# The projection phase of a hybrid encoder layer: new orders around the projections, and squares averaged per head by two single-pass products

## The chip, the core and the metric

The kernel runs on one core of a Trainium2 chip. Five engines work side by side, each through its own queue in order, and wait for one another by semaphores: TensorE (PE) for matrix products, VectorE (DVE), ScalarE (ACT), GpSimd (POOL), and SyncE (SP), which here issues every DMA. The metric is the time of the whole program on the device in microseconds (us).

## The reference, cut to what matters

One encoder layer is applied to a prompt of 1024 tokens and to a sample of 512 tokens, each with 16 learned meta tokens ahead. All in float32, to float32 accuracy.

```python
h = _rmsnorm(x, norm1_g)
proj = h @ w_in                                   # 1024 -> 2304 columns
qa, ka, va, qb, kb, vb = jnp.split(proj, SPLITS, axis=-1)
qa = _rmsnorm(qa.reshape(B, L, NA_HEADS, HEAD_DIM), qn_a_g)   # per head of 64; ka, qb, kb alike
...
mix = jnp.concatenate([_rmsnorm(oa, outn_a_g), _rmsnorm(ob, outn_b_g)], axis=-1)
x = x + mix @ w_out
h = _rmsnorm(x, norm2_g)
x = x + (jax.nn.silu(h @ w_gate) * (h @ w_up)) @ w_down
```

The change is in the projection and in the per-head normalization of queries and keys, which needs the mean of the squares over each head's 64 numbers.

## The kernel before

**Products in three passes.** A float32 number is split into a high part (rounded to the type `fp32r`, in which TensorE makes a product in one pass) and the low rest. `product` (lines 396 to 398) adds high x high, low x high and high x low in a PSUM bank.

**The stages.** A norm phase normalizes and transposes the first 512 tokens and the meta tokens. Then come `project(0)` (these tokens), `project(1)` (prompt tokens 512 to 1023), the prompt's attention, `project(2)` (the sample), the sample's attention, the output projection and the feed-forward network. g is the group of tokens, 0 to 2.

**One group.** `project(g)` has 18 half-steps H. Each takes 128 columns of `w_in` over 512 tokens: 8 x 3 products of 512 columns on PE (in group 0 from H=8 on, 48 smaller ones, since the meta tokens go along). H=0 to 7 are queries; then K and V alternate, H=8 K, H=9 V, and so on to H=16 K, H=17 V. A query or K half-step is "normed":

- ACT `take_out(H)`: waits for PE's half-step H (`mm_done`), makes the high part `wh` of the weights of H+2 (line 1235), waits that DVE has finished H-2 (`normed`), and copies the bank to `raw` and its square to `sq` (lines 1266, 1267).
- POOL `weight_lo`: the low part `wl` of the same weights (line 1044).
- PE `after(g, H)`, after half-step H+1: the head average of the squares, a plain float32 product of `sq` with the 128x128 matrix `head_mean` (line 2203).
- ACT `root(H)`, in half-step H+1 behind that half-step's `take_out`: square root (line 1300).
- DVE `divide(H)`: reciprocal (line 1706), then times `raw` and gain (line 1715).

V half-steps are copied, transposed on PE (lines 2213, 2217) and split; a K is split by `key_high` and `key_low` (lines 1317, 1734) a step later.

**The tokens of the next groups** are prepared inside groups 0 and 1, four tiles x0 to x3 and x4 to x7. In half-steps 0, 2, 4, 6 ACT takes the norm (`x_root`) and DVE scales the tile (`norm_scale`, line 1667), behind that half-step's `divide`. In half-steps 1, 3, 5, 7 PE transposes it (`x_turn`, line 2159), behind `after`, and ACT copies it out. At H=16 of group 0 ACT and DVE split the next group's tokens into `hth` and `htl` (lines 1247, 1740), behind `key_high` and `key_low`.

**Weights** are loaded into two buffers, by SP, when POOL has done the weights before them. The load for H=2 of group 0 stands behind the norm phase's end and the position tables' DMAs.

The order on PE is this loop:

```python
            def project(g):
                for H in range(18):
                    products(g, H)
                    if H:
                        after(g, H - 1)
                    elif g == 1:
                        after(0, 17)
                    n = prepared(g, H)
                    if n is not None and H % 2:
                        x_turn(n)
```

## Time and profile before

| what | value |
|---|---|
| median of 3 runs | 1973.41 us (1971.73 to 1975.48) |
| the profiled execution's own time | 1974.77 us |
| its span, first to last instruction | 1973.0 us |
| mean granted TensorE clock | 0.979 of full |
| PE busy | 1862.0 us, 94% of the span |
| DVE / ACT / POOL busy | 66% / 51% / 48% |
| products of the tokens with the input weights, first to last on PE | 34.0 to 623.7 us, the prompt's attention among it |

The profiled execution is one run and is read instruction by instruction; its span and the 1.8 us around it make its time, which stands 1.4 us above the median. A busy share is an average. What a stage is bound by is seen from its waits: which instruction came last, and whom it held up.

### The profile page before, as it was taken

What the parts mean: (1) busy time and instruction counts of PE and PEld (TensorE: products, weight loads), DVE (VectorE), ACT (ScalarE), POOL (GpSimd) and SP (SyncE); (2) the same over time, 40 slices, a digit from 0 to 9 for tenths busy, and PEclk for the clock granted to TensorE, in tenths of its full rate; (3) what the DMA queues carried; (4) which work ended last, traced back from release to release, by engine and by line L of the source; (5) the groups of instructions that cost most, each with busy time, mean ns of one, the idle gap of its engine ahead of it and who ended that gap; (6) DMA issues with size and microseconds to landing.
All of it is one profiled execution on the core that took longest, in us unless ns stands there. A gap on an engine that the chain in (4) does not pass through costs nothing.

```text
span 1973.0 us, 35334 instructions
## 1 busy us (share of the span) xinstructions
PE 1862.0 (94%) x12047; PEld 1673.4 (85%) x12047; DVE 1298.4 (66%) x2349; ACT 1003.6 (51%) x2085; POOL 953.7 (48%) x807
## 2 busy tenths in 40 slices
PE   5897998999898988997999999999999999999998
PEld 3696777999777876886899999899999989999997
DVE  2556657888666876548666666776666676666664
ACT  3546446888545883345444344544435353444432
POOL 1332335766435652113656464645546464655643
PEclk9999998999998998998999999999999999999999
DMA  4444622444423445011332332343233234323221
GB/s 139 138 134 126 166 85 78 128 126 133 123 77 93 140 119 205 32 54 64 122 114 87 104 106 85 107 172 123 90 106 106 86 107 171 107 92 121 85 85 64
DMA packets 184323, 217.10 MB, mean 110 GB/s; under 512 B 13124, under 2 KB 162100, under 8 KB 183964
## 3 DMA queue, kind: packets, MB, share of 16 engines
q1 hardware_dynamic: 184220, 215.77, 34.9%
q8 instruction: 60, 0.98, 0.2%
q14 instruction: 43, 0.35, 0.1%
HBM read 197.34 MB, written 27.27 MB: 114 GB/s over the span
## 4 chain that ended last, share of the span: by engine, by line
PE 56%; DVE 4%; ACT 2%; issue 2%; POOL 1%; DMA 0%; ACTq 0%; POOLq 0%; DVEq 0%; SPq 0%
PE bank L396 19%; PE bank L397 18%; PE bank L398 18%; DVE mvl L1991 1%; POOL msl L1107 1%; ACT msh L1477 0%; DVE tsum L1987 0%; ACT logit L1383 0%; DVE qm L1888 0%; ACT qm L1407 0%; DVE logit L1813 0%; DMA draw<-in_w_down 0%; DVE pmeta L1828 0%; ACT pth L1392 0%; DVE ptl L1820 0%
## 5 line engine op out<-in xcount | busy, mean ns | idle before, releaser
L396 PE MATMUL bank<-mvh,sth 128*128 128x256 f32 x1848 | 526.2, 285 | 16.3 <-DVE mvl L1991 6.0
L398 PE MATMUL bank<-mvh,stl 128*128 128x256 f32 x1848 | 525.2, 284 | 0.0
L397 PE MATMUL bank<-mvl,sth 128*128 128x256 f32 x1848 | 525.2, 284 | 0.0
L396 PEld LDWEIGHTS bank<-mvh,sth 128*128 128x128 f32 x1848 | 356.6, 193 | 19.6 <-issue 15.0
L397 PEld LDWEIGHTS bank<-mvl,sth 128*128 128x128 f32 x1848 | 357.0, 193 | 1.2
L398 PEld LDWEIGHTS bank<-mvh,stl 128*128 128x128 f32 x1848 | 356.9, 193 | 0.0
L1184 POOL TENSOR_TENSOR dl<-draw,dh 128x1024 fp32r<-128x1024 f32 x66 | 158.2, 2422 | 366.0 <-ACT dh L1570 366.0
L2029 DVE TENSOR_TENSOR y<-bank,y 128x512 f32<-128x512 f32 x264 | 182.4, 692 | 165.4 <-PE bank L398 164.5
L1044 POOL TENSOR_TENSOR wl<-wraw,wh 128x1024 fp32r<-128x1024 f32 x54 | 134.3, 2488 | 269.1 <-ACT wh L1235 269.1
L1178 POOL TENSOR_TENSOR stl<-graw,sth 128x512 fp32r<-128x512 f32 x132 | 177.1, 1343 | 101.8 <-ACT sth L1552 97.5
L396 PE MATMUL bank<-dh,acth 128*128 128x512 f32 x528 | 210.1, 398 | 7.7 <-DVE y L2029 5.3
L397 PE MATMUL bank<-dl,acth 128*128 128x512 f32 x528 | 209.1, 396 | 0.0
L398 PE MATMUL bank<-dh,actl 128*128 128x512 f32 x528 | 208.4, 395 | 0.0
L396 PE MATMUL bank<-hth,wh 128*128 128x512 f32 (+2 forms) x512 | 199.9, 390 | 6.5 <-DVE htl L1740 5.5
L1586 ACT ACTIVATE acth<-act_f 128x512 fp32r<-128x512 f32 x66 | 38.2, 624 | 322.3 <-PE bank L398 314.3
L398 PE MATMUL bank<-hth,wl 128*128 128x512 f32 (+2 forms) x512 | 187.4, 366 | 0.0
L397 PE MATMUL bank<-htl,wh 128*128 128x512 f32 (+2 forms) x512 | 186.4, 364 | 0.0
L1178 POOL TENSOR_TENSOR stl<-uraw,sth 128x512 fp32r<-128x512 f32 x132 | 169.9, 1315 | 5.7 <-ACT sth L1552 5.7
L1235 ACT ACTIVATE wh<-wraw 128x1024 fp32r<-128x1024 f32 x54 | 57.0, 1057 | 188.1 <-PE bank L398 163.6
L1383 ACT ACTIVATE logit<-logit,negm 128x274 f32<-128x274 f32 (+1 forms) x192 | 113.8, 593 | 38.0 <-DVE negm L1813 36.8
L1706 DVE RECIPROCAL rt_p<-rt_p 128x512 f32<-128x512 f32 (+2 forms) x30 | 84.4, 2826 | 67.6 <-ACT rt_p L1300 67.6
L396 PEld LDWEIGHTS bank<-dh,acth 128*128 128x128 f32 x528 | 99.9, 189 | 31.1 <-DVE y L2029 6.5
(247 smaller groups left out, 4293.5 us busy)
## 6 DMA issues: line engine op xcount, KB each, us to landing
graw<-in_w_gate SPq DMA_DIRECT2D x33, 1024.0 KB, 5.4
uraw<-in_w_up SPq DMA_DIRECT2D x33, 1024.0 KB, 5.3
draw<-in_w_down SPq DMA_DIRECT2D x66, 512.0 KB, 4.1
wraw<-in_w_in SPq DMA_DIRECT2D x54, 512.0 KB, 4.0
bias_rows<-table_a SPq DMA_DIRECT2D x36, 192.0 KB, 3.2
out<-y SPq DMA_DIRECT2D x12, 512.0 KB, 3.1
bias<-table_b SPq DMA_DIRECT2D x28, 201.0 KB, 2.6
table_a<-line_a_dram SPq DMA_DIRECT2D x8, 576.0 KB
```

Of the source, the lines that this page charges most:

```text
L396: pe.matmul(out, lhs[0], rhs[0], start=start, stop=False, skip_group_check=True)
L397: pe.matmul(out, lhs[0], rhs[1], start=False, stop=False, skip_group_check=True)
L398: return pe.matmul(out, lhs[1], rhs[0], start=False, stop=stop, skip_group_check=True)
L1044: pool.tensor_tensor(wl[G % 2][:, :, :], wraw[G % 2][:, :, :], f32(wh[G % 2][:, :, :]), ALU.subtract).then_inc(w_lo, 1)
L1107: pool.tensor_tensor(msl[slot][:, :, :], mix_tile(i, slot), f32(msh[slot][:, :, :]), ALU.subtract).then_inc(ms_lo, 1)
L1178: pool.tensor_tensor(stl[:, i, :, :], standing(raw, i), f32(sth[:, i, :, :]), ALU.subtract).then_inc(st_lo_pool, 1)
L1184: pool.tensor_tensor(dl[j][:, :], draw[j][:, :], f32(dh[j][:, :]), ALU.subtract).then_inc(down_lo, 1)
L1235: act.activation(wh[G % 2][:, :, :], wraw[G % 2][:, :, :], ACT.Copy).then_inc(w_hi, 1)
L1383: act.activation(x, x, ACT.Exp, bias=negm[:, h % 2, t:t + 1], scale=-1.0, accum_out=lsum[:, h % 2, t:t + 1]).then_inc(expd, 1)
L1586: act.activation(acth[:, j, :], act_f[:, j, :], ACT.Copy).then_inc(act_hi, 1)
L1706: op = dve.reciprocal(rt[:, u0:u0 + w], rt[:, u0:u0 + w])
L2029: dve.tensor_tensor(yt, DOWN_BANK[half][:, :], yt, ALU.add).then_inc(y_add, 1)
```

## The change

Four things are done.

1. **Squares.** Behind `sq`, ACT copies it to `sqh` in `fp32r`, waiting for its own square first. POOL makes `sql = sq - sqh`, behind its `weight_lo` of the same half-step. PE's head average becomes two `fp32r` products, `sqh` and `sql` with `head_mean_r` (the matrix in `fp32r`; its entries are 0 and 1/64), and waits for `squared_lo`, POOL's result.
2. **Next tokens.** `norm_scale` moves to half-steps 1, 3, 5, 7 in group 0 and 3, 5, 7, 9 in group 1; `x_turn` to the half-step after each, 2 to 8 and 4 to 10. Their loads and the write-back of the turned tiles move along.
3. **Weights.** The loads for half-steps 2 and 3 of group 0 are issued before the norm phase ends, and the first load of each group waits for one buffer only.
4. **The seam between groups 0 and 1.** Of the eight slices of the next tokens' low part DVE makes the even ones and POOL the odd ones, POOL's ahead of its `sql`. `key_high(0, 14)` and `key_low(0, 14)` move between slices 3 and 4.

```diff
@@ -96,6 +96,7 @@
...
     head_mean = r("head_mean", [P, P])
+    head_mean_r = at("head_mean_r", [P, P], F32R, r.offset - P * 4)
     eps = r("eps", [P, 1])
@@ -152,11 +153,13 @@
...
     assert BASE + s.offset <= END
-    sq_of, rt_of = [], []
+    sq_of, sqh_of, sql_of, rt_of = [], [], [], []
     for n, where in (("p", qm_at[2]), ("s", v_at + 4 * 1280 * 4)):
...
         rt_of.append([s(f"rt_{n}{i}", [P, SEG + META]) for i in range(2)])
+        sqh_of.append([s(f"sqh_{n}{i}", [P, SEG + META], F32R) for i in range(2)])
+        sql_of.append([at(f"sql_{n}{i}", [P, SEG + META], F32R, where + i * 4 * (SEG + META)) for i in range(2)])
@@ -431,9 +438,15 @@
...
-        def prepared(g, H):
-
-            return 4 * g + H // 2 if g < 2 and H < 8 else None
+        def squared_x(g, H):
+
+            j = (H - (1, 3)[g]) // 2 if g < 2 and H % 2 else -1
+            return 4 * g + j if 0 <= j < 4 else None
+
+        def turned_in(g, H):
+
+            j = (H - (2, 4)[g]) // 2 if g < 2 and H % 2 == 0 else -1
+            return 4 * g + j if 0 <= j < 4 else None
@@ -450,6 +463,12 @@
...
             return sq_of[g // 2], rt_of[g // 2]
+
+        def squares_split(g, kind):
+            return ([sqh_kv], [sql_kv]) if g and kind == "kvb" else (sqh_of[g // 2], sql_of[g // 2])
+
+        def square_columns(g, kind):
+            return SEG + META if g == 0 and kind != "q" else SEG
@@ -794,23 +813,25 @@
...
             def weight_loads(g):
-                if g == 0:
-                    sp.wait_ge(line_out, 16 * 7)
                 for it in range(1, 9):
+                    if g == 0 and it == 2:
+                        sp.wait_ge(line_out, 16 * 7)
+                        lay_out_a0(0)
                     kind, i = ("q", it) if it < 4 else ("kv", it - 4) if it < 8 else ("kvb", 0)
                     for slot in range(2):
-                        sp.wait_ge(w_lo, 18 * g + it * 2 + slot - 1)
-                        weight_load(kind, slot, i)
-                        if g == 0 and slot == 1:
+                        if g or it > 1:
+                            sp.wait_ge(w_lo, 18 * g + it * 2 + slot - 1)
+                            weight_load(kind, slot, i)
+                        if g == 0 and slot == 1 and it > 1:
                             lay_out_a0(it - 1)
...
                             lay_out_b(2 * it + slot - 2)
-                    if g < 2 and it in (2, 3):
-                        later_x(4 * g + it)
-                    if g == 0 and it in (6, 7):
-                        later_x(it - 2)
-                    if g == 1 and 2 <= it < 6:
-                        keep_turned(it - 2)
+                    if g == 0 and it in (3, 4, 6, 7):
+                        later_x(it - 1 if it < 5 else it - 2)
+                    if g == 1 and it in (4, 5):
+                        later_x(it + 2)
+                    if g == 1 and 4 <= it < 8:
+                        keep_turned(it - 4)
@@ -830,6 +851,9 @@
...
                 norm_rest()
+                for slot in range(2):
+                    sp.wait_ge(w_lo, slot + 1)
+                    weight_load("q", slot, 1)
                 later_x(0)
@@ -955,8 +979,9 @@
...
-            sp.wait_ge(w_lo, 18)
-            first_weights(1)
+            for slot in range(2):
+                sp.wait_ge(w_lo, 17 + slot)
+                weight_load("q", slot, 0)
             weight_loads(1)
@@ -1048,6 +1073,18 @@
...
                         weight_lo(18 * g + H + 2)
+                    if g == 0 and H == 16:
+                        for k in range(1, KT, 2):
+                            pool.wait_ge(h_hi, k + 1)
+                            pool.tensor_tensor(htl[:, k, 0:SEG], qm[:, 1, k, :], f32(hth[:, k, 0:SEG]),
+                                               ALU.subtract).then_inc(h_lo_pool, 1)
+                    if is_normed(H):
+                        kind, i, slot = half_step(H)
+                        w = square_columns(g, kind)
+                        sqh, sql = squares_split(g, kind)
+                        pool.wait_ge(squared_hi, normed_of(g, H))
+                        pool.tensor_tensor(sql[slot][:, 0:w], squares(g, kind)[0][slot][:, 0:w],
+                                           f32(sqh[slot][:, 0:w]), ALU.subtract).then_inc(squared_lo, 1)
@@ -1266,6 +1303,10 @@
...
                     op.then_inc(squared, 1)
+                    act.wait_ge(squared, normed_of(g, H))
+                    w = square_columns(g, kind)
+                    act.activation(squares_split(g, kind)[0][slot][:, 0:w], sq[slot][:, 0:w], ACT.Copy
+                                   ).then_inc(squared_hi, 1)
                     return
@@ -1354,27 +1395,30 @@
...
                         value_high(0, 17)
-                    if H >= 2 and half_step(H - 2)[0] != "q" and slot == 0:
-                        key_high(g, H - 2)
-                    elif g == 1 and H == 0:
-                        key_high(0, 16)
                     if g == 0 and H == 16:
...
                         for k in range(KT):
+                            if k == 4:
+                                key_high(0, 14)
                             if k < KT - 1:
...
                             split_high(1, k)
+                    elif H >= 2 and half_step(H - 2)[0] != "q" and slot == 0:
+                        key_high(g, H - 2)
+                    elif g == 1 and H == 0:
+                        key_high(0, 16)
                     if g and H == 16:
...
                             stage_q(h, False)
-                    n = prepared(g, H)
-                    if n is not None:
-                        x_out(n) if H % 2 else x_root(n)
+                    if squared_x(g, H) is not None:
+                        x_root(squared_x(g, H))
+                    if turned_in(g, H) is not None:
+                        x_out(turned_in(g, H))
@@ -1654,6 +1698,7 @@
...
                     dve.tensor_scalar(gains[:, j:j + 1], gains[:, j:j + 1], SCALE, None, ALU.mult)
+                dve.tensor_copy(head_mean_r[:, :], head_mean[:, :])
                 for k, c0 in enumerate(range(0, LEN_T5, 512)):
@@ -1756,15 +1801,17 @@
...
                         value_low(0, 17)
-                    if H >= 2 and half_step(H - 2)[0] != "q" and H % 2 == 0:
+                    if g == 0 and H == 16:
+                        for k in range(0, KT, 2):
+                            if k == 4:
+                                key_low(0, 14)
+                            split_low(1, k)
+                    elif H >= 2 and half_step(H - 2)[0] != "q" and H % 2 == 0:
                         key_low(g, H - 2)
...
                         key_low(0, 16)
-                    if g == 0 and H == 16:
-                        for k in range(KT):
-                            split_low(1, k)
-                    n = prepared(g, H)
-                    if n is not None and H % 2 == 0:
+                    n = squared_x(g, H)
+                    if n is not None:
                         if n == 0:
@@ -2180,7 +2227,10 @@
...
                             if g and H == 0:
-                                pe.wait_ge(h_lo, 8 * (g - 1) + k + 1)
+                                if g == 1 and k % 2:
+                                    pe.wait_ge(h_lo_pool, k // 2 + 1)
+                                else:
+                                    pe.wait_ge(h_lo, k // 2 + 1 if g == 1 else 4 + k + 1)
                             op = part(k, u0, w, b)
@@ -2189,7 +2239,7 @@
...
                     j = normed_number(g, kind, slot, i)
-                    pe.wait_ge(squared, j + 1)
+                    pe.wait_ge(squared_lo, j + 1)
                     if g == 2 and H == 0:
@@ -2224,9 +2276,8 @@
...
                         after(0, 17)
-                    n = prepared(g, H)
-                    if n is not None and H % 2:
-                        x_turn(n)
+                    if turned_in(g, H) is not None:
+                        x_turn(turned_in(g, H))
                 if g:
```

How that stands on the engines. First ACT, group 0, half-step 3 and the start of the next. `raw`, `sq` are bank and square, `rt` the root, `xs_turned` PE's transposes. Before:

```order
30 L1235 ACTIVATE wh1_79<-wraw1_81 128x1024 [waits w_in1,mm_done]
31 L1266 ACTIVATE raw1_85<-bank1 128x512
32 L1267 ACTIVATE sq_p1_90<-bank1 128x512
33 L1300 ACTIVATE rt_p0_91<-bank4,eps_51 128x512 [waits mean_done]
34 L1341 ACTIVATE qm_62<-bank6 128x4x128 [waits xs_turned]
35 L1341 ACTIVATE qm_62<-bank7 128x4x128 [waits xs_turned]
36 L1235 ACTIVATE wh0_78<-wraw0_80 128x1024 [waits w_in0,mm_done]
```

And now, half-step 2 and the start of the next:

```order
37 L1303 ACTIVATE raw0_85<-bank0 128x512 [waits normed]
38 L1304 ACTIVATE sq_p0_90<-bank0 128x512
39 L1308 ACTIVATE sqh_p0_94<-sq_p0_90 128x512 [waits squared]
40 L1341 ACTIVATE rt_p1_93<-bank5,eps_52 128x512 [waits mean_done]
41 L1382 ACTIVATE qm_63<-bank6 128x4x128 [waits xs_turned]
42 L1382 ACTIVATE qm_63<-bank7 128x4x128 [waits xs_turned]
43 L1272 ACTIVATE wh1_80<-wraw1_82 128x1024 [waits w_in1,mm_done]
```

A copy `sqh` stands between the square and the root of the half-step before; the copy-out of the turned tile has moved by one half-step.

DVE at the start of group 0, before (`line_b` ends the norm phase; L1665 and L1667 are `norm_scale`):

```order
22 L1660 TENSOR_TENSOR line_b<-bank,band 8x14 [waits line_mm]
23 L1665 RECIPROCAL rms<-rms 128x1 [waits rms_done,gs_in,phase_done]
24 L1667 SCALAR_TENSOR_TENSOR spare<-spare,rms 128x2x512 [waits rinv_done]
25 L1706 RECIPROCAL rt_p_91<-rt_p_91 128x512 [waits root_done]
26 L1715 SCALAR_TENSOR_TENSOR qm<-raw_84,gains,rt_p_91 128x512 [waits recip_done]
27 L1706 RECIPROCAL rt_p_92<-rt_p_92 128x512 [waits root_done]
```

And now:

```order
23 L1705 TENSOR_TENSOR line_b<-bank,band 8x14 [waits line_mm]
24 L1751 RECIPROCAL rt_p_92<-rt_p_92 128x512 [waits root_done,phase_done]
25 L1760 SCALAR_TENSOR_TENSOR qm<-raw_85,gains,rt_p_92 128x512 [waits recip_done]
26 L1710 RECIPROCAL rms<-rms 128x1 [waits rms_done,gs_in]
27 L1712 SCALAR_TENSOR_TENSOR spare<-spare,rms 128x2x512 [waits rinv_done]
28 L1751 RECIPROCAL rt_p_93<-rt_p_93 128x512 [waits root_done]
```

The first `norm_scale` now stands behind the first `divide`. From then on one `norm_scale` follows every second `divide`, before and now.

POOL at the seam of groups 0 and 1, now (before, it has only the `wl` there); rows 37 and 38 are the weights of half-step 17 of group 0 and of half-step 0 of group 1:

```order
36 L1086 TENSOR_TENSOR sql_p0_96<-sq_p0_90,sqh_p0_94 128x528 [waits squared_hi]
37 L1069 TENSOR_TENSOR wl1_84<-wraw1_82,wh1_80 128x1024 [waits w_hi]
38 L1069 TENSOR_TENSOR wl0_83<-wraw0_81,wh0_79 128x1024 [waits w_hi]
39 L1079 TENSOR_TENSOR htl_89<-qm_63,hth_88 128x512 [waits h_hi] x4
40 L1086 TENSOR_TENSOR sql_p0_96<-sq_p0_90,sqh_p0_94 128x528 [waits squared_hi]
41 L1069 TENSOR_TENSOR wl1_84<-wraw1_82,wh1_80 128x1024 [waits w_hi]
```

The last `sql` of group 0 (row 40), for which PE's head average of half-step 16 waits, stands behind the four slices of `htl`.

## Rows read from the trace of the kernel before

**Rows 1.** Waits of PE, 30 to 316 us: line, released by, us in total, times, longest.

```profile
PE bank L2159 <- DVE spare L1667: 16.2, 8, 8.3
```

**Rows 2.** Timeline, PE, query half-steps of group 1: start us, us, then [idle before].

```profile
212.18 1.09 PE L2159 MATMUL bank<-ident,spare 128*128 128x128 f32 x8 [1.00 <-DVE spare L1667]
...
218.68 1.02 PE L2203 MATMUL bank<-sq_p,head_mean 128*128 128x512 f32 x2
...
219.77 0.39 PE L397 MATMUL bank<-htl,wh 128*128 128x512 f32 x1
220.00 0.39 PE L398 MATMUL bank<-hth,wl 128*128 128x512 f32 x1
```

**Rows 3.** Timeline, all engines, group 0, from the end of half-step 4.

```profile
78.14 1.02 PE L2203 MATMUL bank<-sq_p,head_mean 128*128 128x512 f32 x2
...
80.26 0.69 ACT L1300 ACTIVATE rt_p<-bank,eps 128x512 f32<-128x512 f32 x1
...
84.37 0.75 DVE L1715 SCALAR_TENSOR_TENSOR qm<-raw,gains,rt_p 128x512 f32<-128x512 f32 x1
84.55 1.02 PE L2203 MATMUL bank<-sq_p,head_mean 128*128 128x512 f32 x2
...
85.23 1.28 DVE L1667 SCALAR_TENSOR_TENSOR spare<-spare,rms 128x1024 f32<-128x1024 f32 x1
...
85.88 2.90 POOL L1044 TENSOR_TENSOR wl<-wraw,wh 128x1024 fp32r<-128x1024 f32 x1 [3.98 <-ACT wh L1235]
...
86.57 1.09 PE L2159 MATMUL bank<-ident,spare 128*128 128x128 f32 x8 [1.00 <-DVE spare L1667]
```

**Rows 4.** A copy to fp32r on ACT (timeline), and POOL's subtraction, min/median/max ns (by tile).

```profile
168.63 4.28 ACT L1247 ACTIVATE hth<-qm 128x512 fp32r<-128x512 f32 x8
...
L1178 POOL TENSOR_TENSOR stl<-graw,sth x132: 1267/1300/2260, 900.3 to 1912.1; 128x512 fp32r<-128x512 f32 x132
```

**Rows 5.** DVE beside a running POOL: timeline of the norm phase, then durations by tile.

```profile
14.35 2.35 POOL L1044 TENSOR_TENSOR wl<-wraw,wh 128x1024 fp32r<-128x1024 f32 x1 [12.85 <-ACT wh L1235]
...
15.86 1.92 DVE L1667 SCALAR_TENSOR_TENSOR xt<-xt,rms,g 128x1024 f32<-128x1024 f32 x1
...
L1734 DVE TENSOR_TENSOR kmeta<-rt_p,kmeta x12: 167/171/2222, 128.2 to 193.4; 64x16 fp32r<-64x16 f32 x12
```

**Rows 6.** Timeline, PE after idle time, and one stretch (busy us by engine, clock, DMA).

```profile
195.17 1.12 PE L2159 MATMUL bank<-ident,spare 128*128 128x128 f32 x4 [8.31 <-DVE spare L1667]
...
203.75 0.59 PE L2203 MATMUL bank<-sq_p,head_mean 128*128 128x512 f32 x1
...
1252.26 0.50 PE L396 MATMUL bank<-dh,acth 128*128 128x512 f32 x1 [2.64 <-DVE y L2029]
...
1599.77 0.80 PE L396 MATMUL bank<-dh,acth 128*128 128x512 f32 x1 [2.65 <-DVE y L2029]
...
196.00:198.00 2.00, 2.00 (x9) 1.81 (x8) 2.00 (x1) 1.19 (x2) 0.00 (x0) 0.50 0.80 264
```

**Rows 7.** Timeline, PE: last product of half-step 1; end of half-step 9, group 0.

```profile
47.41 0.40 PE L398 MATMUL bank<-hth,wl 128*128 128x512 f32 x1
...
114.97 1.05 PE L2203 MATMUL bank<-sq_p,head_mean 128*128 128x256 f32 x4
```

**Rows 8.** Timeline, PE: ends of half-steps 16, 17 (group 0), 0 and 11 (group 1).

```profile
162.47 1.04 PE L2213 MATMUL bank<-ident,raw 128*64 128x128 f32 x8
...
169.30 1.05 PE L2203 MATMUL bank<-sq_p,head_mean 128*128 128x256 f32 x4
...
178.48 0.60 PE L2213 MATMUL bank<-ident,raw 128*128 128x128 f32 x4
...
267.79 0.59 PE L2203 MATMUL bank<-sq_p,head_mean 128*128 128x512 f32 x1
```

**Rows 9.** Timeline, ACT, group 2: `raw` of half-steps 2 and 3.

```profile
531.28 0.60 ACT L1266 ACTIVATE raw<-bank 128x512 f32<-128x512 f32 x1 [0.78 <-DVE qm L1715]
...
537.15 0.60 ACT L1266 ACTIVATE raw<-bank 128x512 f32<-128x512 f32 x1 [0.24 <-DVE qm L1715]
```

16 lines of the change are left out of this document (11 added, 5 removed).

## The prediction, made before the changed kernel ran

> **What bounds the kernel now.** I read the page's busy shares first (PE 94%, so only PE's time counts), then PE's waits, then timelines around its idle stretches. Outside the projections the change touches nothing. Inside them PE runs without a gap but for three kinds of idle time. First, the eight `x_turn` wait for DVE's `norm_scale`, 16.2 us in all, 8.3 of them at one place in group 1 and 1.0 in the steady pairs [rows 1, 2]. Second, 3.4 us and a stretch of half clock after half-step 1, where ACT waited for weights. Third, some 2 us at the seam of groups 0 and 1. The sum below runs from one PE event to another; T is always the moment at which PE ends a half-step's products.
>
> **The head average.** The float32 product starts at 218.68, and the next products keep a spacing of 0.23 us [rows 2]: 219.77 - 0.23 - 218.68 = 0.86 us. Two `fp32r` products of the same width take 2 x 0.23 = 0.46. That saves 0.40 each, 39 times (13 in each group), 15.6 us on PE if PE is what is waited for. The trace has no product of this very operand pair; those of rows 2 have the same type, width and weight load, so I take 0.23, and 0.25 at most.
>
> **What the copy `sqh` adds.** ACT makes eight such copies in 4.28 us, 0.53 apart [rows 4]. Here the copy must also wait for its own square, so it can't overlap it: 0.66, bounds 0.53 and 0.8. It stands between `sq` and `root`, so `root`, `divide` and `norm_scale` come 0.66 later after T. POOL's `sql` takes 1.30 [rows 4] and stands behind `wl`: it ends near T + 5.1, and PE wants it at T + 6.0. That is hidden by the 5.55 us of products, with 0.9 us to spare.
>
> **The turn pairs, the main term.** Before, with T = 78.14 [rows 3]: `root` at T + 2.12, `divide`'s product T + 6.23 to 6.98, `norm_scale` T + 7.09 to 8.37, `x_turn` at T + 8.43. PE ends the next half-step at T2 = 84.55 = T + 6.41 (0.86 + 5.55), and POOL's `wl` starts at T2 + 1.33. Turn and 24 products take 218.68 - 212.18 = 6.50 [rows 2]. The pair of half-steps is 8.43 + 6.50 = 14.93 us.
>
> The change moves `norm_scale` and `x_turn` together, by one half-step in group 0. The distance stays: DVE scales behind the `divide` in the half-step that begins at T, PE turns one half-step later. So the 1.0 us wait is not removed. Now T2 = T + 0.46 + 5.55 = T + 6.01, `wl` is ready at T + 7.34, `divide`'s product runs T + 6.89 to 7.64, and `norm_scale` would start at T + 7.75. The order of the last two has turned over. In rows 3 `wl` came 0.65 after `norm_scale` and took 2.90 instead of its usual 2.4, ending 2.27 after DVE did. When DVE came second, it was held: a `norm_scale` of the norm phase took 1.92 beside POOL's 14.35 + 2.35 = 16.70 and ended 1.08 after it, and a 0.17 us `kmeta` took 2.22 [rows 5]. So `wl` slips in behind `divide`, ends at T + 7.64 + 2.27 = 9.91, and `norm_scale` ends at T + 10.99: `x_turn` at T + 11.05. PE is free for it at T + 6.47 and idles 4.6 us.
>
> A rule that speaks against this change: the Trainium skill (SBUF — State Buffer, "Who interferes with whom") says that a DVE instruction with two SBUF inputs and a GpSimd instruction that reads SBUF exclude each other, and that issue order decides who blocks. Rows 5 agree by their 2.22 and 1.92. If instead the two only slowed each other over their overlap, the turn would be at about T + 10 and the pair 1 us shorter; by the rule it is as computed.
>
> After such idle time the clock is at half. Behind 8.31 us of idle the granted clock was 0.50, 1.2 GHz, and the same turn and 24 products took 203.75 - 195.17 = 8.58 instead of 6.50 [rows 6]: 2.1 more. The pair becomes 11.05 + 8.58 = 19.6 us, against 14.93.
>
> **Sum, piece by piece.**
> (a) Group 0, end of half-step 1 (47.41 + 0.23 = 47.64) to end of half-step 9 (114.97) [rows 7]: 67.3 before. The weights for half-steps 2 and 3 are now there long before, so the wait at 51 us is gone; it cost about 8.7 with its half clock. Now four turn pairs, the last with 0.3 more for the meta columns: 4 x 19.6 + 0.3 = 78.7. That is **+11.4**.
> (b) Half-steps 10 to 16 of group 0: four head averages at 0.4, nothing late: **-1.6**.
> (c) Seam, from the end of half-step 16: before 178.48 - 162.47 = 16.0 [rows 8]. Now POOL makes `wl` (to +3.75), then waits for ACT's second slice (+5.3), makes four slices of 1.3 [rows 4], the last two behind ACT's `key_high`, each blocked a little by DVE's subtractions: they end near +12.1. Only then comes `sql` of half-step 16, +13.4. PE ended half-step 17 at 169.30, +6.83 [rows 8], and its head average comes ahead of group 1. It idles 6.6 us; then 0.46 + 5.55 + 2.1 for the clock: 21.5. **+5.5**. Without any blocking `sql` ends at +11.8, still 5 us late.
> (d) Group 1, end of half-step 0 to end of 11: before 267.79 - 178.48 = 89.3 [rows 8]. DVE is held by `key_low` until +13.3, then each query half-step costs the loop of (e), 6.5: the first `norm_scale`, now behind the third `divide`, ends near +33.1 (the 8.3 us wait becomes several of 0.5 to 2.3 and one of 5.6). 33.1 + 8.58 = 41.7, two pairs 39.2, and 14.5 for the last, where the V half-step has no `sqh`: 95.4. **+6.1**.
> (e) Rest: group 1 saves 3 x 0.4. In group 2 the queries run in a loop: `raw` waits for the `divide` two half-steps back [rows 9], and the next `raw` came 537.15 - 531.28 = 5.87 later, just under PE's 6.41. With `sqh` it is 6.53, over PE's new 6.01: the queries gain nothing. K saves 4 x 0.4. Both attentions begin behind POOL, 0.7 later. **-1.4**.
>
> Total +20.0. On the profiled span of 1973.0 that is 1993.0, with the 1.8 us around it 1994.8; that execution stood 1.4 above the median, so I forecast 1973.4 + 20.0 = **1993.4 us**. At no cost I take: the cast of `head_mean` (DVE waits for PE there), the moved loads of x2 to x7 and the write-backs on SP (each lands some 10 us ahead of its use), and the two early weight loads, which compete with the last token tile (0 +- 1).
>
> **Rivals.**
> (R1) POOL does not get between. It decides within 0.4 us: if `sqh` costs under 0.25, or `wl` is ready after T + 7.75, the turn is at T + 9.1, 2.6 us idle and a pair of 15.6. Then (a) is -4.6, (d) -5.9, the sum -8.0: 1965. But idle times of 2.6 sit where the clock may fall: one of 2.65 in the trace stood beside a fall, one of 2.64 did not [rows 6]. With a fall in all seven the sum is +6.6, 1980; with half, 1973. For R1: in the last pair of group 0 the margin is only 0.1. Against: the copy alone is 0.53.
> (R2) The change does what it is shaped for: squares early enough, no wait at the turns. A pair would be 0.46 + 5.55 + 0.46 + 0.95 + 5.55 = 13.0; (a) -15, (c) -3, (d) -18, all heads 0.4: about 1930. It needs `norm_scale` done by T + 6.47, where rows 3 have 8.37 and the change only adds.
> (R3) The blocking comes but the clock stays up in the seven long waits: -14.6, 1979.
> (R4) POOL's next `sql` also gets ahead of the held `norm_scale`: +1.3 in seven pairs, 2002.
>
> **Chances and range.** The forecast with its neighbours (1984 to 2001) 0.60; between R3 and R1 with clock (1977.5 to 1984) 0.15; within 0.2% (1969.5 to 1977.4), R1 with some falls, 0.10; R1 clean 0.10; R2 0.05. A measurement of this kernel can tell about 0.2%. Faster 0.15, same 0.10, slower 0.75. The range, 1968 to 2001, takes in R3 and most of R1, and leaves out R2 and R4.
>
> **What would show it.** In the trace after: the transposes of `x_turn` wait for `norm_scale` 4 to 5 us in seven places, with the clock at 0.5 behind them, and that `norm_scale` lasts over 3 us; the last head average of group 0 waits 6 us for POOL; group 2's query half-steps are 6.5 apart and its K and V pairs 0.4 shorter. If `norm_scale` shows 1.28 us and the waits are 2.6, R1 is right; if head averages take more than 0.5, the first term is wrong.

## The result, and the profile after

The changed kernel took 2003.49 us (median of 4 runs, 2000.98 to 2003.86); the kernel before, beside it, 1974.32. The ratio is 1.0149, with a 95% interval of 1.0135 to 1.0163: 29 us slower. The forecast was 1993.4, in a range up to 2001: the direction held, and 10 us of the loss were missing from it.

The profiled execution has a span of 2002.1 us against 1973.0, and a mean granted clock of 0.968 against 0.979. PE's busy time hardly differs (1866.7 against 1862.0). PE's waits (line, released by, us in total, times, longest), first 30 to 345 us, then group 2:

```profile
PE bank L2206 <- DVE spare L1712: 28.8, 8, 4.4
PE bank L2253 <- POOL sql_p L1086: 9.7, 2, 6.7
...
PE bank L2253 <- POOL sql_s L1086: 5.6, 8, 1.3
```

The first row answers to [rows 1]: the turns' waits for `norm_scale` grew from 16.2 to 28.8 us. The other two rows are new. PE now waits for POOL's `sql`: at the seam, once in group 1 (3.1 us), and ahead of eight head averages of group 2 (0.25 and 0.76 in turn for most of its queries).

The timeline of a turn pair in group 0, all engines, from the end of half-step 3, answers to [rows 3]:

```profile
67.88 0.40 PE L2253 MATMUL bank<-sqh_p,head_mean_r 128*128 128x512 f32 x1
68.11 0.39 PE L2255 MATMUL bank<-sql_p,head_mean_r 128*128 128x512 f32 x1
...
70.14 0.63 ACT L1308 ACTIVATE sqh_p<-sq_p 128x512 fp32r<-128x512 f32 x1
70.68 0.68 ACT L1341 ACTIVATE rt_p<-bank,eps 128x512 f32<-128x512 f32 x1
...
71.58 1.30 POOL L1086 TENSOR_TENSOR sql_p<-sq_p,sqh_p 128x512 fp32r<-128x512 f32 x1
...
73.92 0.40 PE L2253 MATMUL bank<-sqh_p,head_mean_r 128*128 128x512 f32 x1
...
74.78 0.75 DVE L1760 SCALAR_TENSOR_TENSOR qm<-raw,gains,rt_p 128x512 f32<-128x512 f32 x1
75.25 2.49 POOL L1069 TENSOR_TENSOR wl<-wraw,wh 128x1024 fp32r<-128x1024 f32 x1 [2.36 <-ACT wh L1272]
75.64 3.18 DVE L1712 SCALAR_TENSOR_TENSOR spare<-spare,rms 128x1024 f32<-128x1024 f32 x1
77.69 2.26 POOL L1086 TENSOR_TENSOR sql_p<-sq_p,sqh_p 128x512 fp32r<-128x512 f32 x1
78.88 1.97 PE L2206 MATMUL bank<-ident,spare 128*128 128x128 f32 x8 [4.33 <-DVE spare L1712]
```

T is 67.88. The head average's two products start 0.23 apart. The copy `sqh` stands between square and root. `divide`'s product starts at T + 6.90, POOL's `wl` slips in behind it, and `norm_scale`, 1.28 us of work in [rows 3], takes 3.18 and ends at T + 10.94. PE turns the tile at T + 11.00 after 4.33 us of idle time. These are the predicted steps, and each of the moments that the prediction gives is met to within 0.1 us; the idle time was put at 4.6.

What follows the idle time, in windows of the same kernel (window, its length, busy us and counts of PE, PEld, DVE, ACT, POOL, granted clock, DMA share, GB/s):

```profile
78.00:80.00 2.00, 1.12 (x6) 1.12 (x7) 2.00 (x2) 0.00 (x0) 1.95 (x1) 0.50 0.56 172
80.00:82.00 2.00, 2.00 (x8) 1.71 (x8) 2.00 (x1) 1.20 (x2) 0.00 (x0) 0.50 0.53 161
82.00:84.00 2.00, 2.00 (x6) 1.58 (x5) 0.84 (x2) 0.00 (x0) 0.00 (x0) 0.50 0.01 4
84.00:86.00 2.00, 2.00 (x9) 1.58 (x8) 0.00 (x0) 0.00 (x0) 0.00 (x0) 0.88 0.03 8
```

The clock stays at half, 1.2 GHz, for 5.6 us from the turn on (the last window holds 0.5 us of it). The half clock after the long wait of [rows 6] had cost 2.1 us. There, in the kernel before, the turn began at 195.17 and the clock was back at full in this window, 4.6 us later:

```profile
198.00:200.00 2.00, 2.00 (x6) 1.57 (x6) 1.13 (x2) 0.00 (x0) 0.00 (x0) 0.57 0.78 89
```

Group 2, DVE's multiplication in `divide` and POOL's `wl`, of two half-steps in a row:

```profile
563.56 0.75 DVE L1760 SCALAR_TENSOR_TENSOR qm<-raw,gains,rt_s 128x512 f32<-128x512 f32 x1
...
568.43 2.41 POOL L1069 TENSOR_TENSOR wl<-wraw,wh 128x1024 fp32r<-128x1024 f32 x1 [0.98 <-ACT wh L1272]
...
570.09 1.30 DVE L1760 SCALAR_TENSOR_TENSOR qm<-raw,gains,rt_s 128x512 f32<-128x512 f32 x1
```

`wl` runs from 568.43 to 570.84, and the multiplication beside it takes 1.30 instead of 0.75. The prediction did not have this.

### The profile page after: what moved, and what is told of

It is laid out like the page before. It is cut to its first block, busy times and chain, and to the rows that moved or that the text cites. A ratio compares the mean times of both kernels' runs of the same rounds, so it can differ in the third digit from the quotient of the medians.

```text
span 2002.1 us, 35413 instructions
## 1 busy us (share of the span) xinstructions
PE 1866.7 (93%) x12047; PEld 1686.5 (84%) x12047; DVE 1316.4 (66%) x2346; ACT 1031.3 (52%) x2124; POOL 1014.6 (51%) x850
## 3 DMA queue, kind: packets, MB, share of 16 engines
q1 hardware_dynamic: 184220, 215.77, 34.3%
## 4 chain that ended last, share of the span: by engine, by line
PE 55%; DVE 4%; ACT 2%; issue 2%; POOL 1%; DMA 0%; ACTq 0%; POOLq 0%; DVEq 0%; SPq 0%
PE bank L403 18%; PE bank L404 18%; PE bank L405 18%; DVE mvl L2038 1%; POOL msl L1144 1%; ACT msh L1521 0%; DVE tsum L2034 0%; DVE qm L1935 0%; ACT logit L1427 0%; ACT qm L1451 0%; PE bank L2328 0%; DVE ptl L1867 0%; DVE logit L1860 0%; DVE pmeta L1875 0%; DMA draw<-in_w_down 0%
## 5 line engine op out<-in xcount | busy, mean ns | idle before, releaser
L403 PE MATMUL bank<-mvh,sth 128*128 128x256 f32 x1848 | 526.8, 285 | 16.8 <-DVE act_f L2054 5.6
L403 PEld LDWEIGHTS bank<-mvh,sth 128*128 128x128 f32 x1848 | 357.5, 193 | 19.9 <-issue 16.2
L403 PE MATMUL bank<-hth,wh 128*128 128x512 f32 (+2 forms) x512 | 195.2, 381 | 4.3 <-DVE htl L1785 3.3
L404 PE MATMUL bank<-htl,wh 128*128 128x512 f32 (+2 forms) x512 | 192.0, 375 | 0.0
L405 PE MATMUL bank<-hth,wl 128*128 128x512 f32 (+2 forms) x512 | 191.9, 375 | 0.0
```

What stands on the lines that cost most here:

```text
L403: pe.matmul(out, lhs[0], rhs[0], start=start, stop=False, skip_group_check=True)
L404: pe.matmul(out, lhs[0], rhs[1], start=False, stop=False, skip_group_check=True)
L405: return pe.matmul(out, lhs[1], rhs[0], start=False, stop=stop, skip_group_check=True)
```

## The experiments

The table gives, for each kernel, stretches between events on PE, from its timeline, in us. T1, T9, T16, T17 are the ends of half-steps of group 0. U1, U11 are the first head averages behind half-steps 1 and 11 of group 1. P2 to V17 is group 2, first product to last head average. Time is the median, with its ratio to the runs of the kernel before made on the same chip; T1 to T9 holds the four turns of group 0, U1 to U11 those of group 1.

| kernel | T1-T9 | T9-T17 | T17-U1 | U1-U11 | P2-V17 | span | time | ratio, 95% interval |
|---|---|---|---|---|---|---|---|---|
| before | 67.3 | 54.3 | 16.5 | 82.0 | 114.5 | 1973.0 | 1974.3 | |
| after | 80.9 | 52.9 | 21.3 | 88.6 | 117.9 | 2002.1 | 2003.5 | 1.0149 [1.0135, 1.0163] |
| e1_orders | 60.1 | 54.3 | 18.5 | 79.1 | 114.6 | 1964.7 | 1968.7 | 0.9979 [0.9969, 0.9989] |
| e2_squares | 81.5 | 52.9 | 18.6 | 96.6 | 117.8 | 2008.0 | 2008.6 | 1.0178 [1.0159, 1.0197] |
| e3_copy_later | 60.1 | 52.9 | 20.8 | 76.1 | 119.8 | 1969.2 | 1973.0 | 1.0005 [0.9992, 1.0017] |
| e4_pool_waits | 67.2 | 52.9 | 20.5 | 83.9 | 117.9 | 1981.8 | 1985.2 | 1.0064 [1.0047, 1.0081] |
| e5_fill | 70.8 | 52.9 | 21.0 | 87.2 | 117.9 | 1990.9 | 1991.5 | 1.0102 [1.0077, 1.0128] |
| e7_norm_first | 57.3 | 59.6 | 20.5 | 75.6 | 118.0 | 1971.6 | 1973.2 | 1.0005 [0.9995, 1.0015] |
| e11_old_seam | 80.2 | 52.7 | 16.8 | 91.8 | 117.8 | 1997.4 | 2002.1 | 1.0157 [1.0138, 1.0176] |
| e12_wl_waits_g2 | 80.0 | 52.9 | 21.3 | 88.6 | 113.9 | 1996.0 | 2000.5 | 1.0147 [1.0129, 1.0165] |
| e15_waits_all | 67.0 | 52.9 | 21.2 | 83.7 | 113.9 | 1980.9 | 1982.4 | 1.0047 [1.0032, 1.0061] |
| e13_best | 53.2 | 52.7 | 16.8 | 71.9 | 110.2 | 1948.0 | 1946.7 | 0.9858 [0.9839, 0.9877] |
| e14_f32_best | 55.4 | 54.3 | 13.8 | 69.4 | 114.8 | 1947.7 | 1952.8 | 0.9902 [0.9882, 0.9922] |

A stretch of the table repeats from profile to profile within 1 us where two kernels don't differ in it. A kernel's median stands from 1.3 us below to 5.1 us above the span of its profiled execution, so small effects are read from the stretches.

**Which half of the change costs the time.** `e1_orders` has the new orders, loads and seam without the split squares:

```diff
-                    sqh, sql = squares_split(g, kind)
+                    sq = squares(g, kind)[0]
...
-                        pe.matmul(mb[:, 0:w], head_mean_r[:, :], sqh[slot][:, u0:u0 + w],
-                                  start=True, stop=False, skip_group_check=True)
-                        op = pe.matmul(mb[:, 0:w], head_mean_r[:, :], sql[slot][:, u0:u0 + w],
-                                       start=False, stop=True, skip_group_check=True)
+                        op = pe.matmul(mb[:, 0:w], head_mean[:, :], sq[slot][:, u0:u0 + w],
+                                       start=True, stop=True)
```

> The changed kernel with parts 2 to 4 alone: the squares are not split, the head average is the float32 product again. Which part costs the time? My theory (the copy sqh and the order of POOL's wl and DVE's norm_scale are what costs): without the copy a turn pair is the one of before, 14.9 us, with 1.0 us of idle time at each turn, since the distance from norm_scale to turn is unchanged; the early weights give 8.7, the 8.3 us wait of group 1 is gone (some 6 to 8 with its half clock), the seam is not behind POOL's slices (0 to 2 gained). 1955 to 1962 us in all, 41 to 48 less than after. Group 2 as before. Rival (the new orders themselves cost, whatever the squares do): the turns wait 4 to 5 us here too, over 1985 us.

`e2_squares` is the kernel before with those lines the other way round, the copy `sqh`, POOL's `sql`, and nothing else.

> The kernel before with the split of the squares alone, all orders and loads as before. Theory: norm_scale comes 0.66 later after T, PE's half-step ends 0.40 earlier, so POOL's wl gets ahead of norm_scale in the turn pairs as it does after the change: pairs near 20 instead of 14.9 in group 0 (four of them; in the first, DVE's norm_scale stands ahead of divide) and group 1 (three), that is 6 to 7 x 5, less 39 x 0.4 where PE is what is waited for; group 2's query loop alternates between 6.5 and 7.1 as after the change, so group 2 as a whole is some 4 us longer than before. In all 25 to 35 us slower than before, 1999 to 2010. Rival (the squares' split costs only in the new orders): within 5 us of before, or up to 15 faster.

The orders alone make the kernel faster by 0.1 to 0.3%, the squares alone slower by 1.8%. The pairs are 14.93 us apart in `e1_orders`, exactly as before, with 1.0 us of wait. In `e2_squares` they are 19.5 to 20.2, though `norm_scale` and `x_turn` stand in their old half-steps. DVE and POOL of `e2_squares`:

```profile
71.18 2.49 POOL L1056 TENSOR_TENSOR wl<-wraw,wh 128x1024 fp32r<-128x1024 f32 x1 [2.33 <-ACT wh L1254]
...
71.57 3.19 DVE L1691 SCALAR_TENSOR_TENSOR spare<-spare,rms 128x1024 f32<-128x1024 f32 x1
```

2008.6 lies within what the theory said. The two halves, 5.6 us gained and 34.3 lost, add up to 28.7 of the 29.2. So the loss belongs to the squares, and moving the turns neither caused nor cured it. My 1955 to 1962 for `e1_orders` was too hopeful. The early weights gave 7.2 us in T1 to T9 (8.7 expected), but its seam is 2.0 longer than before, and the first turn of group 1 still waits 5.3 us. At the seam PE waits for a slice of `htl`, since DVE's and POOL's slices hold each other up:

```profile
162.72 3.24 POOL L1079 TENSOR_TENSOR htl<-qm,hth 128x512 fp32r<-128x512 f32 x2 [0.86 <-ACT hth L1277]
...
164.84 3.44 DVE L1767 TENSOR_TENSOR kmeta<-rt_p,kmeta 64x16 fp32r<-64x16 f32 x2
...
169.06 0.50 PE L403 MATMUL bank<-hth,wh 128*128 128x512 f32 x1 [4.13 <-DVE htl L1773]
```

Two slivers of `kmeta` that take 0.35 us when DVE is alone take 3.44 here. Part 4 of the change thus costs time even without `sql` behind it.

**What holds `norm_scale`.** `e3_copy_later` moves ACT's copy behind the root of the half-step before:

```diff
-                    act.wait_ge(squared, normed_of(g, H))
-                    w = square_columns(g, kind)
-                    act.activation(squares_split(g, kind)[0][slot][:, 0:w], sq[slot][:, 0:w], ACT.Copy
-                                   ).then_inc(squared_hi, 1)
                     return
...
+                    if is_normed(H):
+                        square_high(g, H)
```

`square_high` holds the four lines, and stands behind `finish(g, H - 1)`.

> The changed kernel with ACT's copy sqh moved behind the root of the half-step before it (and what goes with that root); nothing else. Theory: root, divide and norm_scale come 0.66 us earlier; norm_scale is to start at T + 7.1 with POOL's wl ready at T + 7.34, so DVE is first and is not held: x_turn at T + 8.4, 1.9 idle, pair 14.9 to 15.0 (17.0 if the clock falls behind 1.9 us). Seven pairs x 3 to 5 us. sql comes some 0.7 to 1.5 later, and PE's head average may now wait a little for it. Group 2's loop goes back to 5.9 to 6.1 a half-step, 6 to 8 us less than after in the group. In all 1955 to 1975. Rival (the 0.66 us don't decide; the order of wl and norm_scale stays): the pairs keep 20 us and only group 2 gains, 1993 to 1999.

DVE and POOL in the pair that begins at T = 62.19, and PE's turn:

```profile
69.27 1.28 DVE L1720 SCALAR_TENSOR_TENSOR spare<-spare,rms 128x1024 f32<-128x1024 f32 x1
...
69.56 3.26 POOL L1069 TENSOR_TENSOR wl<-wraw,wh 128x1024 fp32r<-128x1024 f32 x1 [2.36 <-ACT wh L1272]
...
70.61 1.09 PE L2214 MATMUL bank<-ident,spare 128*128 128x128 f32 x8 [1.76 <-DVE spare L1720]
```

`norm_scale` starts at T + 7.08, 0.29 us ahead of `wl`. Now it is `wl` that is held (3.26 for 2.4), the turn comes at T + 8.42, the clock stays full, and the pair is 14.94. A lead of 0.3 us instead of a lag of 0.4 is worth 5 us a pair. But group 2 did the opposite of what I expected, 119.8 instead of less: `sql` became later, and `wl` there holds every query's multiplication (1.4 and 2.4 us in turn instead of 0.75), so the half-steps are 6.50 and 7.55 apart in turn. 1973 lies just inside what the theory said.

`e4_pool_waits` leaves the copy where the change put it, and takes the collision away instead:

```diff
                 for H in range(18):
+                    if turned_in(g, H) is not None:
+                        pool.wait_ge(xn_done, 5 + turned_in(g, H) + 1)
                     if H < 16 or g == 0:
                         weight_lo(18 * g + H + 2)
```

> The changed kernel where POOL, in the half-steps with a turn, waits for the norm_scale of that tile before it makes wl. This takes the order of wl and norm_scale away as a cause and leaves the copy sqh where it is. Theory (POOL holds DVE): norm_scale lasts 1.28 us again and ends at T + 9.05, x_turn at T + 9.1, 2.6 us idle. Pair 15.6 if the clock stays up, 17.7 if it falls behind 2.6 us: the seven pairs give 32 or 17 us back, 1971 or 1986. Group 2 is untouched: its 4.3 us over before stay. Rival (norm_scale is late for another reason, such as the copy alone): pairs of 20 us, 2003.

```profile
70.00 1.29 DVE L1714 SCALAR_TENSOR_TENSOR spare<-spare,rms 128x1024 f32<-128x1024 f32 x1
...
71.34 0.90 PE L2208 MATMUL bank<-ident,spare 128*128 128x128 f32 x3 [2.43 <-DVE spare L1714]
...
71.36 2.38 POOL L1069 TENSOR_TENSOR wl<-wraw,wh 128x1024 fp32r<-128x1024 f32 x1 [4.11 <-DVE spare L1714]
```

With T = 62.25 the turn is at T + 9.09, as the first rival had it, and the wait is 2.4 us. 1985 is the value expected for the case that the clock falls behind each (1986). It did at six of the eight turns; the pairs behind it are 17.1 to 17.2 us, and one behind 2.49 us of idle time, with the clock up, is 15.6. So a fall costs 1.5 us here, less than the 2.1 expected. Taking the hold on DVE away gives back 18 us, part of it as shorter stretches of half clock, and no work was taken away for it.

**What the clock costs.** `e5_fill` puts 18 more products ahead of each wait:

```diff
                 g = n // 4
+                wait(pe, staged, 2 * n - 1 if n % 4 else 0)
+                for r in range(18):
+                    pe.matmul(turn_banks(g)[0][:, :], hth[:, r & 7, 0:P], hth[:, r & 7, 0:SEG],
+                              start=True, stop=True, skip_group_check=True)
                 pe.wait_ge(xn_done, 5 + n + 1)
```

> The changed kernel with 18 more products of 512 columns (4.1 us at full clock) on PE ahead of each of the eight waits for norm_scale, into the bank that the transposes then overwrite: they change no result and keep PE busy where it idled 4.3 us. This prices the clock by itself. Theory (the rest of a pair's cost, some 2.5 us beyond the wait, is the half clock behind the idle time): the clock stays up, a pair of group 0 takes 11.1 + 6.5 = 17.6 us instead of 19.8 to 20.7, PE having more work and the kernel less time: six or seven pairs x 2.3 to 3, less some 5 us where the idle time was shorter than the 4.1 us put in (two places of group 1): 1989 to 1995. Rival (24 products take 2 us more for another reason, such as DMA or the PSUM): the pairs stay at 20 us or grow by what is put in, 2003 to 2012.

PE does 33 us of useless work more, and the kernel is 12 us faster than the changed one. The pairs of group 0 take 17.57, 17.57 and 17.73 us, against 19.76, 20.10 and 20.42. The difference, 2.2, 2.5 and 2.7, is what the half clock costs a pair; 17.57 is 11.05 + 6.50 of the prediction to 0.02. Windows of `e5_fill` from the second turn (76.35) on, with the granted clock at 1.00:

```profile
76.00:78.00 2.00, 1.74 (x13) 1.52 (x13) 2.00 (x2) 0.96 (x2) 1.43 (x1) 1.00 0.74 190
78.00:80.00 2.00, 2.00 (x10) 1.64 (x9) 1.97 (x2) 0.12 (x1) 0.00 (x0) 1.00 0.25 72
```

**The miss in group 2.** `e12_wl_waits_g2` lets POOL wait for the divide two half-steps back, in group 2 alone:

```diff
+                    if g == 2 and H >= 2 and is_normed(H - 2):
+                        pool.wait_ge(normed, normed_of(g, H - 2))
                     if H < 16 or g == 0:
                         weight_lo(18 * g + H + 2)
```

> The changed kernel where POOL, in group 2 alone, waits before each wl for the divide two half-steps back, the same that ACT's raw waits for. It tells where the miss in group 2 comes from (+3.4 us from first product to the last head average, where -0.9 was forecast). Theory (POOL's wl holds DVE's divide in every second half-step: its product lasts 1.30 and 0.75 in turn, and the head averages are 6.55 and 7.07 apart): the product takes 0.75 each time and the spacing is 6.5 throughout, 2 us less than after in group 2, 2001.5 in all (seen in the trace, hardly in the time). Rival (the spacing of 7.07 is POOL's own chain wl, sql, for which PE waits 0.76): wl starts later, sql ends later, and the spacing stays or grows: 2003 to 2006.

The multiplications of the eight queries by tile (ns min/median/max, first and last start), first of the changed kernel, then of this run:

```profile
L1760 DVE SCALAR_TENSOR_TENSOR qm<-raw,gains,rt_s x8: 753/1039/1983, 555.8 to 604.4; 128x512 f32<-128x512 f32 x8
```

```profile
L1762 DVE SCALAR_TENSOR_TENSOR qm<-raw,gains,rt_s x8: 752/752/753, 554.2 to 600.0; 128x512 f32<-128x512 f32 x8
```

No multiplication is held any more. The query half-steps are 6.01 and 6.85 us at the start and 6.51 to 6.56 from there on (45.56 us for the first seven, against 47.31), and the group takes 113.9 instead of 117.9. That is 4.0 of the 5.0 us by which the group was missed, twice what I expected of this run. In the whole time so little can't be told (1.0147 against 1.0149). `e15_waits_all` has these waits in all groups, and those of `e4_pool_waits`.

> The changed kernel where POOL waits before each wl for the divide two half-steps back, in all groups, and in the half-steps with a turn for that tile's norm_scale too. No engine's order of work is changed. Theory (POOL's wl beside DVE's two-operand instructions is the whole of the loss but for the seam, the copy and the clock): the run with the waits at the turns alone gave -18 to -20 us against after, the one in group 2 alone -4.0 in that group; they add to 24, 1979 to 1981. No two-operand product of DVE lasts over 0.9 us in the query half-steps. Rival (they don't add, because a wl that waits makes sql and so PE wait): 1984 to 1990, with new waits of PE for sql.

Group 2 is 113.9 again. The turns came out as in `e4_pool_waits`, 67.0 and 83.7: outside group 2 the waits for `divide` added nothing. No multiplication of a query takes over 0.8 us, as the theory had it, and 1982 us is just above its 1979 to 1981. A ratio of 1.0047 (before: 1) leaves 0.5%. I put that down to the copy, the seam and the half clock; this run does not take them apart.

**The seam.** `e11_old_seam` undoes part 4 in the changed kernel:

```diff
                     if H < 16 or g == 0:
                         weight_lo(18 * g + H + 2)
-                    if g == 0 and H == 16:
-                        for k in range(1, KT, 2):
-                            pool.wait_ge(h_hi, k + 1)
-                            pool.tensor_tensor(htl[:, k, 0:SEG], qm[:, 1, k, :], f32(hth[:, k, 0:SEG]),
-                                               ALU.subtract).then_inc(h_lo_pool, 1)
...
+                    if g == 0 and H == 16:
+                        for k in range(KT):
+                            split_low(1, k)
```

> The changed kernel with its part 4 undone: DVE makes all eight slices of the next tokens' low part, behind key_low, ACT's key_high stands ahead of its eight slices, as before the change; POOL makes wl and then sql of half-step 16 at once. The squares are split and the other orders are new. In the run without the squares' split the seam, end of half-step 16 of group 0 to end of half-step 0 of group 1, took 18.9 us against 16.0 before, so the new order of the slices costs 2.9 even without sql behind it. Theory: PE's head average of half-step 16 no longer waits 6.65 us; the seam goes from 22.15 to about 16 us: 6 less than after, 1997. In group 1 DVE is free a little earlier or later, 0 to 2. Rival (the seam needs DVE's relief, and DVE's eight slices make PE wait at the first products of group 1): 19 to 22 us, 2000 to 2004.

The 6.6 us wait for `sql` is gone and T17 to U1 is 4.5 us shorter, but U1 to U11 is 3.2 longer. There `wl` now meets the multiplication ahead of the first `norm_scale` of group 1, and the turn waits 5.14 us with the half clock behind it, where it had waited 1.9:

```profile
222.37 2.34 POOL L1068 TENSOR_TENSOR wl<-wraw,wh 128x1024 fp32r<-128x1024 f32 x1 [1.59 <-ACT wh L1266]
...
223.40 1.85 DVE L1752 SCALAR_TENSOR_TENSOR qm<-raw,gains,rt_p 128x512 f32<-128x512 f32 x1
...
226.70 1.97 PE L2196 MATMUL bank<-ident,spare 128*128 128x128 f32 x8 [5.14 <-DVE spare L1704]
```

The time is that of the changed kernel (1.0157 and 1.0149, intervals that overlap), not the 1997 of the theory, and not for the rival's reason either: DVE's eight slices hardly make PE wait (1.0 and 1.3 us). The seam's loss is real where it stands and mostly given back later; as a repair by itself it is worth nothing that the time shows.

**Norm first.** `e7_norm_first` moves one call on each of two engines in the changed kernel:

```diff
                     kind, i, slot = half_step(H)
+                    if squared_x(g, H) is not None:
+                        x_root(squared_x(g, H))
                     take_out(g, H)
...
+                    n = squared_x(g, H)
+                    if n is not None:
+                        if n == 0:
+                            dve.wait_ge(gs_in, 16)
+                        norm_scale(5 + n, P, xs[n % 2], g1s)
                     if H:
                         finish(g, H - 1)
```

> The changed kernel with x_root ahead of take_out on ACT and norm_scale ahead of the divide on DVE, in the same half-steps: the tile is there long before the turn. All else is as in after, the copy sqh and the seam too. Theory: no turn waits, no idle time and no half clock; a pair is PE's own 0.46 + 5.55 + 0.46 + 0.95 + 5.55 = 13.0 us, unless the loop raw, sq, sqh, root, divide (6.5 to 6.8 a half-step here, as in group 2, plus norm_scale's 1.28 in every second) sets it: 13.1 to 14.8. Seven pairs of 20.2 become 13.0 to 14.8, 38 to 50 us less than after: 1953 to 1966. Rival (the lock moves elsewhere: POOL's wl now meets norm_scale or divide at another place and the loop eats the gain): pairs of 16 and more, over 1975.

No turn waits for `norm_scale` any more, and the first pair is 13.06 us. The next are 16.59 and 14.27, and the V and K half-steps behind them, T9 to T17, take 59.6 instead of 52.9. At 1973 us it falls between theory (up to 1966) and rival (over 1975). The gain was eaten as the rival said, seen in six multiplications that start between 67 and 129 us (2.18, 2.92, 2.43, 1.53, 1.67 and 2.50 for 0.75 to 0.90), all beside a `wl`. What is late by it holds PE: ahead of the third turn PE waits 2.37 us for `sql`, with the clock at half behind that, and behind two V half-steps 2.2 us for DVE. The second of the six, and PE's wait:

```profile
75.49 2.42 POOL L1069 TENSOR_TENSOR wl<-wraw,wh 128x1024 fp32r<-128x1024 f32 x1 [2.59 <-ACT wh L1272]
...
75.54 2.92 DVE L1760 SCALAR_TENSOR_TENSOR qm<-raw,gains,rt_p 128x512 f32<-128x512 f32 x1
...
81.63 0.79 PE L2253 MATMUL bank<-sqh_p,head_mean_r 128*128 128x512 f32 x1 [2.37 <-POOL sql_p L1086]
```

**A version faster than both.** `e13_best` puts the edits of `e3_copy_later`, `e7_norm_first` and `e11_old_seam` together and lets POOL wait in all groups:

```diff
                 for H in range(18):
+                    if squared_x(g, H) is not None:
+                        pool.wait_ge(xn_done, 5 + squared_x(g, H) + 1)
+                    if H >= 2 and is_normed(H - 2):
+                        pool.wait_ge(normed, normed_of(g, H - 2))
```

> All that the runs pointed to, on top of the changed kernel: norm_scale and x_root first in their half-step, the copy sqh behind the root, POOL's wl waiting for the divide two half-steps back (and for norm_scale where there is one), the seam's slices as before the change. Theory (then PE is the bound throughout the projections): pairs with a turn 13.0 us, query half-steps 6.01 apart in all groups, no wait of PE over 1 us in the projections but at the seam. First product of group 2 at about 476 to 482 us, where the kernel before has 509, and group 2 another 3 shorter: 1936 to 1945. Rival (ACT's or DVE's own work a half-step, or the sql behind the waiting wl, is now the bound: the loop is over 6.5): 1955 to 1965.

`e14_f32_best` is the same without the split, with the copy and `sql` gone and the float32 head average back:

> The same without the split of the squares: the head average is the float32 product, there is no sqh or sql. New orders, norm_scale first, POOL's wl waiting, the seam's slices as before. It tells what the split is worth once nothing holds DVE. Theory: a pair with a turn is 0.86 + 5.55 + 0.86 + 0.95 + 5.55 = 13.8 us, query half-steps are 6.41 apart; the first wait of group 1 (5.3 us in the run with the orders alone) and its half clock are gone: first product of group 2 near 484 to 488, 1946 to 1952 in all. The split's own worth is then the difference to the run beside it, 39 x 0.4 less what its copies cost: 5 to 15. Rival (the split is worth nothing because ACT and POOL then bind): both runs within 3 us.

Both beat the kernel before, by 1.4% and 1.0%; group 2 begins at 486.2 and 482.6 us (509.2 before), 4 us later and 1 earlier than expected. Both times, 1946.7 and 1952.8, stand 1 to 2 us above what the theories gave. In `e13_best` the first two pairs of group 0 are 12.95 us (the third is 14.10, the three of group 1 12.94 to 13.41), and group 2's queries are 6.06 apart, PE's own work; every query's multiplication takes 0.75, in group 2:

```profile
L1764 DVE SCALAR_TENSOR_TENSOR qm<-raw,gains,rt_s x8: 750/752/753, 507.6 to 548.7; 128x512 f32<-128x512 f32 x8
```

What the split is worth then: 4.5 us in group 2, 2.2 in group 0's turns and 1.6 in T9 to T17, but the seam is 3.0 and U1 to U11 2.5 longer with it, where PE waits 4.40 us for `sql`. The spans of the profiled executions are equal (1948.0 and 1947.7), while the medians are 6 us apart and the ratios 0.4%, with intervals that don't overlap. So the split is worth somewhere between nothing and 9 us, and these runs don't settle how much; 5 to 15 was expected.

## Why the prediction was right, and where it was wrong

The profiled execution is 29.1 us longer; the forecast had 20.0. (The remaining 1.0 us of the miss is that the profiled run of before lay 1.4 above the median of 1973.4 from which the forecast starts, and this one 0.4 above its own.) By its own pieces:

| piece | forecast | measured |
|---|---|---|
| end of half-step 1 | 0 | +0.4 |
| (a) T1 to T9 | +11.4 | +13.6 |
| (b) T9 to T16 | -1.6 | -1.6 |
| (c) T16 to end of half-step 0 | +5.5 | +6.1 |
| (d) to end of half-step 11 | +6.1 | +5.4 |
| (e) rest | -1.4 | +5.2 |

**The head average**: right, 0.23 between its two products, and PE's half-step is 6.04 in the rows above, for 6.01.

**The copy `sqh`**: right. From the square's start to the root's it is 1.16 us in the changed kernel (69.52 to 70.68) and 0.48 before (79.78 to 80.26): 0.68 more, taken as 0.66.

**POOL's `sql`**: called hidden, with 0.9 us to spare. In the turn pairs it is (it ends at T + 5.0, taken as 5.1). In group 1 the one wait of 5.6 of (d) came as 3.09 for `sql` and 1.93 for the turn, and in group 2 PE waits for `sql` 5.6 us in all. There it was not hidden, since `raw` starts late.

**The turn pair**: the order of `wl` and `norm_scale` turned over as worked out, and `x_turn` stood at T + 11.0. `e3_copy_later` and `e4_pool_waits` show both halves of that argument: who comes first at the port decides, and the decision hangs on 0.4 us. The rule from the Trainium skill (SBUF — State Buffer, "Who interferes with whom") holds: the shared port pair is an exclusive lock, and who issues first decides who is blocked. The trace has `norm_scale` at 3.18, the 2.10 that `wl` still had to run plus its own 1.28, less 0.2 of overlap. The same section says that a DVE instruction with at most one SBUF input, outside the two-port modes, doesn't contend; the trace agrees, the reciprocal of 128x512 takes 3.35 us beside a `wl` or a `sql` as without one.

**The clock term**: mis-sized. I took the 2.1 us of one place in group 1, where the half clock lasted 4.6 us from the turn on; at the four turns of group 0 it lasted 4.9 to 6.0, and `e5_fill` shows 2.2 to 2.7 us for it. The four pairs cost 10.1 us more than in `e5_fill` (80.9 against 70.8), for 8.3 taken: 1.8 of the 2.2 us missing in (a). That the clock falls at all seven turns was right.

**The seam**: the wait of 6.6 us for `sql` came as worked out. But the text blames it alone for the 5.5. `e1_orders` shows that the new slices cost 2.0 even without it, and `e11_old_seam` that 3.2 of what the seam costs is bought back in group 1. The step that put nothing on PE's own wait for DVE's and POOL's slices was wrong, without harm to the sum, since PE waits longer for `sql`.

**Group 2, in (e), is where the prediction failed.** It is 5.0 of the 9.1 us missing; without it the time would have been within the range. The step reads: "With `sqh` it is 6.53, over PE's new 6.01: the queries gain nothing". The loop of 6.53 is there when nothing is held (6.51 to 6.56 in `e12_wl_waits_g2`). But I moved the loop by 0.66 and did not ask, as I had for the turns, where POOL's `wl` would then stand against `divide`. Before, PE at 6.41 was slower than the loop at 5.87. After the first two half-steps ([rows 9]) `raw` waited no more, and the multiplication was over when `wl` came, here by 0.76 us:

```profile
548.29 0.75 DVE L1715 SCALAR_TENSOR_TENSOR qm<-raw,gains,rt_s 128x512 f32<-128x512 f32 x1
...
549.80 2.42 POOL L1044 TENSOR_TENSOR wl<-wraw,wh 128x1024 fp32r<-128x1024 f32 x1 [4.01 <-ACT wh L1235]
```

Now PE is faster than the loop, in each second half-step `wl` comes ahead of the multiplication (568.43 and 570.09 in the rows above), and that multiplication is held. Measured: +3.4 against -1.6 for the group, 4.0 of it shown to be `wl`. The loop alone, 45.56 us for seven half-steps over the 44.86 of before, is 0.7 more.

**Smaller**: from the end of group 1 to group 2 it is +1.8 (forecast +0.7), and behind group 2 +1.2 (+0.7). Most of it is PE's wait for `raw` of the last V: 2.1 us in group 1, where the kernel before and `e1_orders` have 0.7, and 1.3 in group 2, where they have none. The rest is no more than the attention's stretch differs between profiles.

**The rivals.** R1 is what `e4_pool_waits` brings about, at T + 9.1; left alone it did not happen. R2 needs the four edits of `e13_best`, and even with them the time is 1947, not some 1930. R3 is `e5_fill` but for the filler's price. R4 did not happen: in the rows of the pair above `sql` comes to the port at 77.69 and takes 2.26, waiting for `norm_scale`, not the other way.

## What to carry to other kernels

When an edit speeds up the engine that paces the kernel, ask of each pair of engines that share something (here DVE's two-operand instructions and POOL) who comes first afterwards, in every loop and not only where a wait shows already. A small shift can turn their order over, and a waiting semaphore on the engine that has slack (POOL's `wl`, needed two half-steps later) puts it right: 18 us at the turns and 4.0 in group 2. It is not quite free: in `e15_waits_all` the wait for `sql` at the start of group 1 is 3.6 us, for 3.1. Price a saving of 0.4 us on the bound engine together with what its copies add to the chain that feeds it.
